# The row stores of the chunk stage, issued by GpSimd in place of SyncE

## The reference

```python
def step(s, xt):
    wt, kt, vt, kkt, at = xt[:5]
    sa = jnp.einsum('bhvk,bhk->bhv', s, -kkt)
    s = (s * wt[:, :, None, :] + sa[..., None] * (kkt * at)[:, :, None, :]
         + vt[..., None] * kt[:, :, None, :])
    return s, jnp.einsum('bhvk,bhk->bhv', s, xt[5])
```

## Time and profile before

| | |
|---|---|
| median of 3 runs | 4237.51 us (4225.91 to 4882.52) |
| profiled execution, its own time | 4227.41 us |
| its span | 4225.6 us |
| its mean granted clock of TensorE | 0.936 |

### The profile page before, as it was taken

The page is one execution under the profiler, slowest core; times in us unless marked ns, Lnnn a source line. Parts: engine busy times, 40 slices in busy tenths (PEclk is TensorE's granted clock), DMA queues, the critical chain, the costliest instruction groups (busy, mean ns, idle before and its releaser), DMA issues. The chain is left out here.

```text
span 4225.6 us, 94312 instructions
## 1 busy us (share of the span) xinstructions
PE 3688.7 (87%) x39674; PEld 3082.4 (73%) x39674; DVE 2139.4 (51%) x3448; ACT 1842.5 (44%) x2997; POOL 714.9 (17%) x901
## 2 busy tenths in 40 slices
PE   7999999999977767676778779999399999999993
PEld 6777878778766667666667667778388888888883
DVE  5552543643525545454445785454554445454445
ACT  6543544533424444443445544343144444444443
POOL 1110010110102222222222133400011111111111
PEclk8999999999988888888889989999599999999997
DMA  7666565555544222323231456564466666656667
GB/s 261 196 211 201 180 222 152 178 174 156 182 129 103 76 74 72 78 71 78 67 107 38 136 181 223 175 215 145 161 210 211 216 210 218 209 209 211 221 213 288
DMA packets 450626, 702.99 MB, mean 166 GB/s; under 512 B 189400, under 2 KB 328256, under 8 KB 432720
## 3 DMA queue, kind: packets, MB, share of 16 engines
q1 hardware_dynamic: 416416, 587.26, 43.5%
q0 software_dynamic: 33840, 110.40, 8.5%
HBM read 531.97 MB, written 165.56 MB: 165 GB/s over the span
## 5 line engine op out<-in xcount | busy, mean ns | idle before, releaser
L113 PE MATMUL fro__acc<-fro__hT_hi,fro__wh 128*128 128x512 f32 (+1 forms) x1608 | 629.8, 392 | 12.6 <-DVE fro__hT_lo L2676 8.9
L114 PE MATMUL fro__acc<-fro__hT_hi,fro__wl 128*128 128x512 f32 (+1 forms) x1608 | 615.1, 383 | 0.0
L115 PE MATMUL fro__acc<-fro__hT_lo,fro__wh 128*128 128x512 f32 (+1 forms) x1608 | 614.8, 382 | 0.0
L2006 DVE TENSOR_TENSOR fin__wl<-fin__raw,fin__wh 128x4096 fp32r<-128x4096 f32 x96 | 424.7, 4424 | 317.1 <-ACT fin__wh L1950 317.1
L2682 DVE TENSOR_TENSOR fro__wl<-prj__w,fro__wh 128x1024 fp32r<-128x1024 f32 x201 | 246.3, 1225 | 586.7 <-ACT fro__wh L2419 586.5
L1950 ACT ACTIVATE fin__wh<-fin__raw 128x4096 fp32r<-128x4096 f32 x96 | 348.5, 3630 | 191.1 <-PE exp__acc L115 190.3
L113 PE MATMUL exp__acc<-fin__wh,exp__xh 128*128 128x512 f32 x1024 | 399.9, 391 | 0.7 <-DVE exp__xl L2011 0.7
L115 PE MATMUL exp__acc<-fin__wl,exp__xh 128*128 128x512 f32 x1024 | 398.5, 389 | 0.0
L114 PE MATMUL exp__acc<-fin__wh,exp__xl 128*128 128x512 f32 x1024 | 398.5, 389 | 0.0
L113 PEld LDWEIGHTS fro__acc<-fro__hT_hi,fro__wh 128*128 128x128 f32 x1608 | 305.5, 190 | 87.3 <-issue 31.5
L115 PEld LDWEIGHTS fro__acc<-fro__hT_lo,fro__wh 128*128 128x128 f32 x1608 | 305.4, 190 | 59.2
(11 more groups left out here) (467 smaller groups left out, 7617.9 us busy)
## 6 DMA issues: line engine op xcount, KB each, us to landing
fin__raw<-in_w_x SPq DMA_DIRECT2D x96, 2048.0 KB, 7.6
prj__w<-in_w_z SPq DMA_DIRECT2D x201, 512.0 KB, 4.1
s_zT<-fro__pool SPq DMA_DIRECT2D x128, 256.0 KB, 4.5
fro__wm<-in_w_mod POOLq DMA_DIRECT2D x16, 1024.0 KB, 6.2
mix__gate<-s_zT SPq DMA_DIRECT2D x64, 256.0 KB
prj__xin<-in_tokens SPq DMA_DIRECT2D x18, 512.0 KB, 5.5
rwc__bon<-s_bon SPq DMA_DIRECT2D x36, 256.0 KB
s_y<-rwc__yo SPq DMA_DIRECT2D x144, 64.0 KB, 2.1
```

The source lines that it names most:

```text
L113: pe.matmul(out, sh, mh, start=first, stop=False)
L114: pe.matmul(out, sl, mh, start=False, stop=False)
L115: return pe.matmul(out, sh, ml, start=False, stop=last)
L2006: ve.tensor_tensor(wl[s][:, :, :], raw[s][:, :, :], wh[s][:, :, :], ALU.subtract).then_inc(w_lo, 1)
```

## The change

`store_rows` moves from SyncE's list to GpSimd's, with its waits and its two DMAs unchanged. GpSimd issues half 1 of slab h - 2 behind `rho(h + 1)` and half 0 of slab h - 1 at the end of its round; three more calls stand behind its loop for the last slabs. The wait for the last landings at the end of the stage moves too.

```diff
@@ SyncE
-            def store_rows(j, t):
-                s = turn_of(j, t)
-                sp.wait_ge(S[f"yc{t}"], at(f"yc{t}", j))
-                heads = T["y"][j % 2, ds(slab_at(j) + HC * s, HC), :].rearrange("t (q e c) -> t e q c", q=4, e=2)
-                for e in range(2):
-                    sp.dma_start(heads[:, e, :, :], yo[t][side(e ^ s), :].rearrange("t (q c) -> t q c", q=4)).then_inc(y_out[t], 16)
...
                 if h < SLABS:
                     store_bonus(h)
-                if exists(h - 3):
-                    store_rows(h - 3, 1)
-                if exists(h - 2):
-                    store_rows(h - 2, 0)
...
-            for t in range(2):
-                sp.wait_ge(y_out[t], 32 * SLABS + START)
             sp.wait_ge(b_out, 16 * SLABS + START)
@@ GpSimd
+            def store_rows(j, t):
+                s = turn_of(j, t)
+                gp.wait_ge(S[f"yc{t}"], at(f"yc{t}", j))
+                heads = T["y"][j % 2, ds(slab_at(j) + HC * s, HC), :].rearrange("t (q e c) -> t e q c", q=4, e=2)
+                for e in range(2):
+                    gp.dma_start(heads[:, e, :, :], yo[t][side(e ^ s), :].rearrange("t (q c) -> t q c", q=4)).then_inc(y_out[t], 16)
...
                     rho(h + 1)
+                if exists(h - 2):
+                    store_rows(h - 2, 1)
                 residue(h, 0)
                 residue(h, 1)
                 rounded_inverse(h)
+                if exists(h - 1):
+                    store_rows(h - 1, 0)
+            store_rows(LAST - 1, 1)
+            store_rows(LAST, 0)
+            store_rows(LAST, 1)
+            for t in range(2):
+                gp.wait_ge(y_out[t], 32 * SLABS + START)
```

## The result

| | before | after |
|---|---|---|
| median | 4231.7 us (4 runs, 4225.8 to 4882.5) | 4032.4 us (4 runs, 4030.6 to 4037.1) |
| ratio, 95% interval | | 0.9535 (0.9514 to 0.9557) |
| profiled execution | 4227.4 us, span 4225.6 | 4037.1 us, span 4035.3 |

The change made the kernel 4.65% faster. One execution of the kernel before was slow, at 4882.5 us, and the ratio leaves it out. The forecast of 3996 us was 36 us too low, inside its range of 3955 to 4055 and outside the likeliest case's own range, which ended at 4015.

What follows compares the result with a forecast made beforehand. ScalarE's wait at `yo` for stores SyncE issued late was taken to bound the chunk stage. From 4227.4 us, less 231 (30 rounds) and 1 (round 2), plus 1 (stage end), came 3996 us, range 3955 to 4055.

Steps and rivals of the forecast that it cites:

- What bounds the kernel: Chunk stage: ScalarE waits 218.5 us at `yo` for stores that SyncE issues late, behind 19 loads.
- What is removed: ScalarE's wait for row stores: 7.24 us in each of 30 rounds, and 1.31 us in round 2.
- What the round becomes: Rounds 3 to 32 fall from 30.49 to 22.8 us, between 23.25 and 21.55, gaining 231 us.
- the one on the loads: Loads beside the new rounds: judged by round 2's 23.07 us, they take the round from 22.7 to 22.8 us.
- The clock: TensorE's work after the wait runs at full clock again, giving back 0.57 us a round.
- What GpSimd pays: Store issues at 0.6 us each, 1.2 us a pair, hidden in rooms of 6.6 and 8.8 us.
- What SyncE keeps: Loads and bonus store, a 16.4 us pass; the bonus store lands at 17.8 us, wanted at 22.8, margin 5 us.
- The end of the stage: The chunk stage's last stores, now GpSimd's, land later than from SyncE; 1 us lost.
- Rounds like those without loads: Rival, 12%: the chunk stage's rounds fall to 21.55 us, time 3959 us.
- SyncE as the bound: Rival, 12%: SyncE's load issue stretches to a pass of 22 us, round 24.8, time 4056 us.
- GpSimd as the bound: Rival, 2%: GpSimd's issues outgrow their room; at 9 us a DMA the round is 34.2, time about 4338 us.
- Nothing changes: Rival, 4%: stores land late from any queue, or the loads' arrival sets the round; about 4227 us.

Runs made afterwards that it cites:

- e1: Kernel before, with the row stores kept on SyncE but issued ahead of the round's waits and loads; 4013.7 us, ratio 0.9491.
- e4: Kernel before, with two `yo` tiles per half and the stores left behind the loads on SyncE; 4011.0 us, ratio 0.9485.
- e5: Changed kernel with only half 1's stores moved to GpSimd, half 0's left on SyncE behind loads and bonus store; 4029.9 us, ratio 0.9530.
- e6: Changed kernel with only half 0's stores moved to GpSimd, half 1's left on SyncE behind the bonus store; 4229.1 us, ratio 0.9996.
- e2: Changed kernel with loads of slabs 3 to 35 cut to 16 partitions, same number of DMAs, outputs differ; 3979.4 us, one run.
- e12: e1 with loads cut to 16 partitions from slab 3 on, outputs differ; 3965.1 us, one run.
- e10: e1 plus four needless stores a round issued by GpSimd at the changed kernel's two places; 4016.5 us, ratio 0.9505.
- e7: Changed kernel with each row store cut into four DMAs, 16 a round on GpSimd for the same bytes; 4051.7 us, ratio 0.9579.
- e11: e1 plus four needless stores a round issued by SyncE behind the bonus store; 4014.5 us, ratio 0.9492.

## Why the prediction was right, and where its sum was off

**What bounds the kernel.** Right. The wait for `yo[1]` was on the path of every round, SyncE's order made the store late, and e1, e4, e5 and e6 each show it from another side: other place, other buffer, that half, and not the other half.

**What is removed.** Right: 217 us of waiting are gone in 30 rounds, and none came back in another wait on a DMA.

**What the round becomes.** This is the term that was mis-sized: 22.8 us a round forecast, 23.82 measured, so 231 us were counted and 200 came. I bounded the round by 23.25 (the wait alone) and 21.55 (no loads, no wait), and the result lies outside both. The step that failed is the one on the loads. I took their cost from round 2, let them add 0.1 us to the 22.7 that the wait and the clock left, and took 23.25 as the upper end because a wait that goes can't cost more than it lasted. They added 1.7 us of pauses. The wait of some 7 us had covered pauses beside the loads. In round 14 of the kernel before TensorE stood still from 1724.96 on, for 6.9 us, while SyncE still issued loads until 1727.46 and they went on landing. As in the earlier trace rows:

```profile
1725.00:1731.80 6.80, 0.00 (x0) 0.00 (x0) 0.00 (x0) 0.95 (x4) 0.00 (x0) 0.78 0.40 99
```

No matmul, and transfers that held 0.40 of the DMA engines, at 99 GB/s. Over the 30 rounds the standstills covered 31% of the bytes moved. Without the wait, TensorE works through all of the loads. The standstill began 12.8 us into a round on average: behind that point the pauses rose from 0.2 to 1.15 us a round, which the covering explains. In the first 12.8 us they rose too, from 0.8 to 1.5 us, and why is not shown. That the loads cause the pauses is shown by e2 and e12 (pauses 1.0 and 0.9, rounds 1.7 and 1.3 us shorter), and the path is the fetching of TensorE's instructions, by the packets above. Where a packet is held up beside the loads, at the DMA engines or in the memory, stays open.

The other two terms were off as well, and partly in the other direction. The clock went back to 1.00 as forecast, but gave 1.5 us a round and not 0.57, which I had taken from one stretch of one round. The standstill gave 6.8 and not 7.24. Against the forecast that is +0.4 for the standstill, -0.9 for the clock and +1.6 for the loads, together +1.0. So the total came as near as it did partly by luck.

**What GpSimd pays.** Right in price, 0.62 us an issue against 0.6, and in effect: hidden, by e10. With 4.2 us a pair, in e7, nearly so.

**What SyncE keeps.** Right: no new wait for `s_bonus`. The store is issued 14.8 us into the round in the median, 0.9 us earlier than I had, and lands 3.2 us later, where I had 2.1; ScalarE wants it at 23.1. The margin is the 5 us of the forecast. e11, whose pass is some 6 us longer than the changed kernel's, doesn't test it, as its additions stand behind the bonus store.

**The end of the stage.** One us counted, 2.6 measured. In the changed kernel the last copy and the next stage's first instruction on ScalarE are

```profile
2141.93 0.38 ACT L359 ACTIVATE rwc__yo<-rwc__PB 128x256 f32<-128x256 f32 x1 [0.78 <-PE rwc__PB L796]
...
2148.06 0.21 ACT L2940 ACTIVATE hold__lgr<-hold__lgr 128x8 f32<-128x8 f32 x1 [5.74 <-PEq L64]
```

6.1 us apart, and 3.5 us (2335.48 to 2339.00) in the kernel before; e1, with the stores on SyncE, has 3.5 too.

**The rivals.** Rounds like those without loads: excluded, by 23.82 against 21.55. (Round 33 itself, forecast to stay at 21.6, took 22.49.) SyncE as the bound: not seen. (A pass of 22 us would give 22 + 0.6 + 2.1 = 24.7 by the prediction's own sum, not 24.8, and 4054 us.) GpSimd as the bound: not seen even at four times the issues. Nothing changes: false.

**The warning weighed in the prediction** (Trainium skill, SBUF — State Buffer, "SBUF: two separate sides"), that VectorE can hold up the descriptors of a DMA issued by GpSimd: no such hold shows here. 144 issues lay between 582 and 639 ns, and the median landing was 2.3 us, the longest 6.8, against 2.1 and 4.0 from SyncE. It is a weak test: of VectorE's instructions beside these issues nearly all had two inputs, and only four were casts. The hold of 8 us that the prediction let fit would have missed its room: 1.2 + 8 is more than 8.8.

**What stays open.** The changed kernel is 19 us slower than e1. Of these 2.6 us are the end of the stage, and four needless stores on GpSimd cost 3 us, within the noise. A round of the changed kernel is 0.54 us longer than e1's, and its pauses are 0.54 us longer, so they are the whole of it; that its `beta` product takes 0.24 us more doesn't show in TensorE's other idle time. What makes its instructions come later than e1's is not settled: e5, e7 and e10 have GpSimd's DMAs too, and pauses like e1's, with one profiled execution of each.

## What to carry to other kernels

If an engine waits for a short DMA, look at what the issuing queue did in the microseconds before it: a store of 2 us that is issued behind 16 us of loads is a store of 18 us. The cheapest cure is to put it ahead of the wait that the queue stands in anyway, or to give its source a second buffer; another engine's queue works as well, but not better. And a wait that covers everything hides other stalls too: the round less the wait is no upper end for the new round, as the stalls that the idle engines would have met in that time are still to come.

## What the runs showed of the hardware

- An issue on SyncE's queue depends on its size: about 0.6 us over 64 or 128 partitions, 0.43 us over 16. The load pass of 19 DMAs took 15.7 us with full tiles and 11.2 us with 16 partitions of each.
- TensorE runs out of instructions beside loads from HBM. Its pauses without a named releaser were 2.7 us a round at full load traffic and 1.0 at a small one, in pieces of up to 2.1 us, and each of them (90 and 56) ended 1.1 to 1.65 us after a 16 KB packet of instructions had landed.
- GpSimd issues a DMA of 64 by 4 pieces of 256 bytes in 0.62 us and one of 64 single pieces in 0.52 us: four times the pieces cost 0.1 us more.
